# Attention of the first block's layers: V stationary for two heads at once in column halves, outputs turned, probabilities scaled ahead

## The chip, the cores and the metric

The kernel runs on one core of one Trainium2 chip. The metric is the device time of one execution in microseconds; the time given for a kernel is the median of its runs. Of the kernel before there are 3 runs: 1504.77, 1504.91 and 1505.8 us.

## The reference, cut to what matters

Two blocks of two layers each run over 256 rows of 1024 channels, all in float32. The change touches the attention of the first block's two layers (`hybrid_mixer`). There 16 heads of 64 channels stand behind 8 heads that only choose keys: 6 heads of kind A (the best 64 of the keys by those scores), 5 of kind B (a banded mask with a bias), 5 of kind C (a forgetting mask).

```python
def hybrid_mixer(h, cos, sin, w_in, b_in, rel_bias, w_branch, w_out):
    proj = h @ w_in + b_in
    ...
    o_a = dsa_attention(qa, ka, va, qi, ki, wi)
    o_b = chunk_band_attention(qkv_b[:, :, 0], qkv_b[:, :, 1], qkv_b[:, :, 2], rel_bias)
    o_c = forgetting_attention(qkv_c[:, :, 0], qkv_c[:, :, 1], qkv_c[:, :, 2], f_c)
    gates = jax.nn.sigmoid(gate_logits.reshape(B, S, N_BRANCH, D))
    y = (gates[:, :, 0] * (o_a @ w_branch[:WIDTH_A])
         + gates[:, :, 1] * (o_b @ w_branch[WIDTH_A:WIDTH_A + WIDTH_B])
         + gates[:, :, 2] * (o_c @ w_branch[WIDTH_A + WIDTH_B:]))
    return y @ w_out

# each of the three attentions ends so:
    p = jax.nn.softmax(logits, axis=-1).astype(v.dtype)
    out = jnp.einsum('bhqs,bshd->bqhd', p, v)
```

## The kernel before, in words

Rows stand on partitions: 256 rows are two row tiles of 128. Every product with a large weight matrix goes through units. A unit is up to two k-tiles of 128 x 512 weights. SP brings it into a ring of 8 raw buffers, ACT rounds it into a high part (line 1180), POOL subtracts to get the low part (line 674), and PE multiplies three times for each k-tile and row tile: high part of the input by high weights, low by high, high by low (line 716). PE says `unit_used` when it is done, and ACT may run 5 units ahead of PE. SP's order is one list, and PE, ACT, POOL and DVE each run a list of their own with semaphore waits between them.

The attention of a layer is one loop over k (function `attention`, once for each engine), with 24 heads: 8 of kind I, then 5 B, 5 C and 6 A. The dictionary ONE holds its distances: a head h is scored in iteration h+1, its probabilities are turned and weighed with V in iteration h+3. In an iteration PE does, in this order: for even h the score products of two heads (lines 925 and 928, each head on 64 of the 128 array rows); for even k the turning of the queries and keys of the next two heads (line 943); `turn_head` of head k-3, three transposes of its exponentials into a bank (line 904); `weave`, one gate unit of the large products for k up to 23 and branch units for k = 24 to 26; and `weigh_head` of head k-3 (lines 891 to 893). That last one has the turned probabilities as the stationary operand, 128 columns, and 64 columns of V moving, three products for a head, the results in columns 384 to 511 of the same bank.

ACT in an iteration: `prep`, one unit's high part; for (k-6) a multiple of 4 the tanh of a gate chunk; for even k the copy of the turned queries and keys (line 1288); the exponentials of head k-1 in two instructions with their row sums (lines 1300, 1302).

DVE in an iteration: adds mask and scales for head k-1 (lines 1731, 1732), copies the turned probabilities of head k-3 from the bank to SBUF (line 1705); for k a multiple of 4 drains a gate chunk (two adds of 128 x 512); for k = 10 to 17 one round of the choice of the largest 8 (lines 1931 to 1934); and `put_out`: the reciprocal of the row sums (line 1748, for two heads at once) and the product of the head's output with it into `o_rows` (line 1750, 128 x 128). PE's transposes of the following head wait for `head_out`, which this last product gives, since they write the same bank.

The outputs are needed turned, since they are the input of the branch products. `turn_heads` (line 1050) does that with 16 transposes for a layer, in iterations 21, 23, 25, 26 (the dictionary BRANCH_TURNS) and after the loop, each group followed by `heads_hi` on ACT (line 1267) and `heads_lo` on DVE (line 1890), which split it into a high and a low part in `branch_turned` (kinds B and C) or `turned` (kind A).

POOL has, beside the low parts, in layer 0 a modulation sum after every fourth unit (lines 651, 655).

The second block's attention uses the same functions with the dictionaries TWO and other distances.

Of the kernel before, what the change touches and what calls it, by code (L numbers as in the profile page):

```python
# [29 lines left out]
P = 128  # L30
# [69 lines left out]
BRANCH_TURNS = {21: 0, 23: 1, 25: 2, 26: 3}  # L100
# [235 lines left out]
def program(nc, ctx, dram, out, cat, book):  # L336
# [37 lines left out]
    O, _ = place("o_rows", [P, NT, D])  # L374
# [46 lines left out]
    BT, _ = place("branch_turned", [P, 6, 2, S], F32R, at=mb_at)  # L421
    assert mb_at + 6 * 2 * S * 4 <= cm_at + HC * 3 * P * 4
# [39 lines left out]
    ONE = dict(score=1, turn=3, weigh=3, qk=QKT, pt=PT, n_pt=2, n_qk=2, sb=(SB_,), tp=(TP,) * (HI + HB + HC + HA - 2) + SB_, act_copies=False)  # L462
    TWO = [dict(score=3, turn=5, weigh=7, qk=QKT2, pt=PT2, n_pt=3, n_qk=3, sb=(SB_, (0, 2)), tp=tp, act_copies=True)
# [11 lines left out]
    LAST_OF_TURN = (HI + HB + HC - 1,) * 3 + (N_HEADS - 3, N_HEADS - 1)  # L475
# [38 lines left out]
    headed = signal("headed")  # L514
    head_out = signal("head_out")
# [165 lines left out]
    def _(pe):  # L681
# [19 lines left out]
        def unit(c, i, A, tiles=range(NT)):  # L701
# [8 lines left out]
            for m, (a, b) in enumerate(nt):  # L710
                for q, (part, W) in enumerate(((0, HI_), (1, HI_), (0, LO))):
# [3 lines left out]
                    for t in tiles:  # L715
                        ins = pe.matmul(BANK[2 * c["pair"] + t][:, 0:w], A[:, a, part, t * P:(t + 1) * P], W[:, s, b, 0:w],  # L716
                                        start=(i == 0 and m == 0 and q == 0),
                                        stop=(i == len(c["units"]) - 1 and m == len(nt) - 1 and q == 2))
# [160 lines left out]
        def attention(tag, heads, src, weave, pipe):  # L879
# [27 lines left out]
            for k in range(len(heads) + pipe["weigh"]):  # L907
# [22 lines left out]
                if k < len(heads) and k % 2 == 0:  # L930
# [4 lines left out]
                    if one["kind"] == "A" and k - 1 in BRANCH_TURNS:  # L935
                        pe.wait_ge(turned_lo.sem, turned_lo.at((("o", tag), BRANCH_TURNS[k - 1])))
# [8 lines left out]
                if pipe["turn"] == pipe["weigh"]:  # L945
# [54 lines left out]
        for l in range(DEPTH):  # L1000
# [31 lines left out]
            def weave(k, l=l):  # L1032
                if 3 <= k < 3 + HC + 1:
                    forget_products(l, k - 3)
                if k in BRANCH_TURNS:
                    turn_heads(l, BRANCH_TURNS[k])
                if k < 4 * N_GATE:
                    unit(by_key["gate", l, k // 4], k % 4, HT)
# [3 lines left out]

            def turn_heads(l, n):

                pe.wait_ge(head_out.sem, head_out.at((l, LAST_OF_TURN[n])))
                if n:
                    pe.wait_ge(turned_lo.sem, turned_lo.at((("o", l), n - 1)))
                for m, kt in enumerate(((6, 7), (4, 5), (3,), (0, 1), (2,))[n]):
                    for t in range(NT):
                        ins = pe.transpose(BANK[TQ][:, (m * NT + t) * P:(m * NT + t + 1) * P], O[:, t, kt * P:(kt + 1) * P], con("ident"))  # L1050
                ins.then_inc(turned.sem, turned.mark((("o", l), n)))

            def branch_unit(l, cc, b, u):

                pe.wait_ge(turned_lo.sem, turned_lo.at((("o", l), {"C": (1, 0), "B": (2, 1), "A": (3, 4)}[b][u])))
# [23 lines left out]
            turn_heads(l, 4)  # L1079
# [68 lines left out]
    def turned_parts(n):  # L1148

        return ((((BT, 4, 2, 0, P), 0),), (((BT, 1, 1, 0, P), 0), ((BT, 2, 1, 0, DH), 1), ((BT, 3, 1, DH, P), 1)),  # L1150
                (((BT, 0, 1, 0, P), 0),), (((HT, 0, 2, 0, P), 0),), (((HT, 2, 1, 0, P), 0),))[n]
# [15 lines left out]
    def _(act):  # L1167
# [95 lines left out]
        def heads_hi(l, n):  # L1263
# [964 lines left out]
```

## Time and profile before

| | |
|---|---|
| median of 3 runs | 1504.91 us (1504.77 to 1505.8) |
| the profiled execution | 1503.01 us, its span 1501.2 us |
| PE busy | 1464.6 us, 98% |
| DVE, ACT, POOL busy | 771.3, 717.7, 1204.2 us |
| attention loop of layer 0 | about 121 to 235 us in the span |
| attention loop of layer 1 | about 563 to 677 us in the span |
| granted TensorE clock, mean | 0.995 |

The busy share is the time in which an engine has an instruction under way; matmuls are pipelined and their ends are modelled, so a PE that waits a few tenths of a microsecond can still show as busy. Between instructions of the timeline the starts are the safer measure. A float32 matmul of 128 or 256 columns appears as two records, a product of rounded operands or a transpose as one.

### The profile page before, as it was taken

To read this page: it belongs to the slowest core of one execution; us is meant where nothing else is said; L and a number is where in the kernel's file an instruction comes from. 1 tells how busy PE (TensorE), PEld (TensorE's weight loads), DVE (VectorE), ACT (ScalarE), POOL (GpSimd) and SP (SyncE) were. 2 spreads that over 40 slices of the span, in tenths; PEclk is the share of its full clock that TensorE was granted. 3 is DMA by queue.
4 is the path that set the end of the run, shared out by engine and by line. 5 is a ranking of instruction groups with operands and counts; after the bars stand their busy time and mean duration, and the time that the engine had idled before them with its cause. 6 is when DMAs were issued, how large, how long until landed. Compare 5 with 4: busy or idle time off the path is not lost.

```text
span 1501.2 us, 21800 instructions
## 1 busy us (share of the span) xinstructions
PE 1464.6 (98%) x7762; PEld 1237.0 (82%) x7762; DVE 771.3 (51%) x1594; ACT 717.7 (48%) x1154; POOL 1204.2 (80%) x968
## 2 busy tenths in 40 slices
PE   7999999999999999999999999999999999999997
PEld 3898888799978987888788887878888887788886
DVE  7667755666643758655566304264650044555302
ACT  3435554544444444554544444364654345455432
POOL 4799989788878986648898997917999978279994
PEclk9999999999999999999999999999999999999999
DMA  9994546589875995326676565724555657156551
GB/s 354 389 338 169 185 168 215 203 295 330 303 261 169 400 315 168 116 94 203 217 244 204 190 200 165 217 74 137 190 194 196 222 156 225 43 163 202 196 193 60
DMA packets 149685, 313.88 MB, mean 209 GB/s; under 512 B 10933, under 2 KB 31817, under 8 KB 149577
## 3 DMA queue, kind: packets, MB, share of 16 engines
q1 hardware_dynamic: 147824, 311.15, 61.9%
q8 instruction: 62, 1.02, 0.3%
q10 hardware_dynamic: 1754, 1.35, 0.3%
q14 instruction: 45, 0.37, 0.1%
HBM read 311.39 MB, written 1.06 MB: 208 GB/s over the span
## 4 chain that ended last, share of the span: by engine, by line
PE 90%; DVE 5%; ACT 2%; POOL 1%; issue 1%; DMA 0%; SPq 0%; DVEq 0%; ACTq 0%
PE bank L716 56%; PE bank L759 12%; PE bank L760 8%; PE bank L757 5%; PE bank L904 2%; PE bank L925 1%; POOL lo_units L674 1%; PE bank L893 1%; PE bank L892 1%; PE bank L891 1%; PE bank L943 1%; DVE bank L1508 1%; ACT hi_units L1180 1%; PE bank L795 1%; PE bank L847 1%
## 5 line engine op out<-in xcount | busy, mean ns | idle before, releaser
L674 POOL TENSOR_TENSOR lo_units<-raw_units,hi_units 128x512 fp32r<-128x512 f32 (+3 forms) x928 | 1154.0, 1281 | 261.8 <-ACT hi_units L1180 260.5
L1180 ACT ACTIVATE hi_units<-raw_units 128x1024 fp32r<-128x1024 f32 (+1 forms) x470 | 483.2, 1031 | 431.5 <-PE bank L716 274.6
L716 PE MATMUL bank<-hi_units,turned 128*128 128x512 f32 (+3 forms) x1600 | 438.8, 389 | 1.5 <-DVE turned L1556 1.2
L716 PEld LDWEIGHTS bank<-hi_units,turned 128*128 128x128 f32 x1600 | 295.0, 189 | 51.9 <-DVE turned L1556 1.8
L760 PE MATMUL bank<-turned,lo_units 128*128 128x256 f32 x1024 | 288.2, 281 | 0.0
L716 PE MATMUL bank<-hi_units,turned_wide 128*128 128x512 f32 x992 | 274.5, 391 | 0.0
L759 PE MATMUL bank<-turned,hi_units 128*128 128x512 f32 x736 | 260.6, 399 | 0.0
L716 PE MATMUL bank<-lo_units,turned 128*128 128x512 f32 (+3 forms) x800 | 253.3, 384 | 1.5 <-POOL lo_units L674 1.3
L716 PEld LDWEIGHTS bank<-hi_units,turned_wide 128*128 128x128 f32 x992 | 185.3, 188 | 38.5 <-issue 0.5
L760 PEld LDWEIGHTS bank<-turned,lo_units 128*128 128x128 f32 x1024 | 194.2, 190 | 0.2
L716 PEld LDWEIGHTS bank<-lo_units,turned 128*128 128x128 f32 x800 | 150.5, 189 | 31.4 <-POOL lo_units L674 4.8
L759 PEld LDWEIGHTS bank<-turned,hi_units 128*128 128x128 f32 x736 | 138.3, 188 | 34.3
L716 PE MATMUL bank<-lo_units,turned_wide 128*128 128x512 f32 x496 | 160.6, 389 | 0.0
L1508 DVE SCALAR_TENSOR_TENSOR bank<-ada_units,small,bank 128x512 f32<-128x512 f32 x144 | 108.8, 756 | 34.7 <-DMA ada_units<-in_ada_w 30.2
L716 PEld LDWEIGHTS bank<-lo_units,turned_wide 128*128 128x128 f32 x496 | 93.1, 188 | 19.5
L1574 DVE TENSOR_REDUCE bank<-bank 128x256 f32<-128x512 f32 x92 | 64.4, 700 | 86.5 <-PE bank L760 85.6
L757 PE MATMUL bank<-turned,hi_units 128*128 128x256 f32 x576 | 104.0, 283 | 0.0
L757 PEld LDWEIGHTS bank<-turned,hi_units 128*128 128x128 f32 x576 | 90.2, 192 | 0.6
L1300 ACT ACTIVATE scores<-scores,small 128x128 f32<-128x128 f32 x60 | 24.0, 400 | 57.9 <-DVE small L1732 57.3
L2035 DVE SCALAR_TENSOR_TENSOR bank<-x_rows,bank 128x512 f32<-128x512 f32 x8 | 5.2, 693 | 89.7 <-PE bank L716 89.7
L1441 ACT ACTIVATE mlp_relu<-bank 128x256 f32<-128x256 f32 x56 | 21.6, 386 | 60.5 <-DVE bank L1574 59.9
L1570 DVE TENSOR_TENSOR turned_wide<-bank,turned_wide 128x256 fp32r<-128x256 f32 x92 | 39.1, 425 | 15.5 <-ACT turned_wide L1214 12.7
(249 smaller groups left out, 1375.5 us busy)
## 6 DMA issues: line engine op xcount, KB each, us to landing
ada_units<-in_ada_w SPq DMA_DIRECT2D x88, 512.0 KB, 7.4
raw_units<-in_w_ffn_tiles SPq DMA_DIRECT2D x72, 512.0 KB, 5.3
raw_units<-in_mlp_w_out SPq DMA_DIRECT2D x64, 512.0 KB, 3.3
raw_units<-in_mlp_w_tiles SPq DMA_DIRECT2D x56, 512.0 KB, 3.3
raw_units<-in_w_in SPq DMA_DIRECT2D x56, 458.0 KB, 9.7
raw_units<-in_w_in SPq DMA_DIRECT2D x48, 512.0 KB, 6.5
raw_units<-in_w_ffn_out SPq DMA_DIRECT2D x44, 512.0 KB, 3.9
raw_units<-in_moba_w_qkv SPq DMA_DIRECT2D x24, 512.0 KB, 3.7
```

Of the source, the lines that this page charges most:

```text
L674: pool.tensor_tensor(LO[:, s, b, 0:w], RAW[:, u["slot"], b, 0:w], HI_[:, s, b, 0:w].bitcast(F32), ALU.subtract).then_inc(lo_ready.sem, lo_ ...
L716: ins = pe.matmul(BANK[2 * c["pair"] + t][:, 0:w], A[:, a, part, t * P:(t + 1) * P], W[:, s, b, 0:w], start=(i == 0 and m == 0 and q == 0) ...
L757: pe.matmul(bank[:, 0:S], HI_[:, s, b, at:at + P], A[:, kt, part, :], start=kt == 0 and part == 0, stop=False)
L759: pe.matmul(bank[:, :], HI_[:, s, b, at:at + P], A[:, kt, :, :].rearrange("p two s -> p (two s)"), start=kt == 0, stop=False)
L760: ins = pe.matmul(bank[:, 0:S], LO[:, s, b, at:at + P], A[:, kt, 0, :], start=False, stop=kt == KT - 1)
L904: ins = pe.transpose(bank[:, at:at + P], SM[:, h % N_SM, cols], con("ident"))
L1180: act.activation(HI_[:, s, 0:n, 0:w], RAW[:, u["slot"], 0:n, 0:w], ACT.Copy)\
L1300: act.activation(SM[:, h % N_SM, S:S + P], SM[:, h % N_SM, S:S + P], ACT.Exp, bias=NM[:, m:m + 1], scale=-1.0, accum_out=RS[:, m:m + 1])
L1441: act.activation(RTN[:, m % 4, :], BANK[(TQ, TP)[m % 2]][:, 0:S], ACT.Relu).then_inc(act_side.sem, act_side.mark(("relu tile", i, m)))
L1508: ins = v.scalar_tensor_tensor(total, raw[:, k, :], COND[:, kt:kt + 1], partial, ALU.mult, ALU.add)
L1570: tell(v.tensor_tensor(AT[:, n, 1, :], h, AT[:, n, 0, :].bitcast(F32), ALU.subtract), turned_lo, (tag, "tile", n))
L1574: return v.tensor_reduce(to, bank[:, :].rearrange("p (two s) -> p s two", two=2), AX_X, ALU.add)
```

## The change

The products with V swap their operands. V's 64 columns of a head are stationary and the turned probabilities move: for a pair of heads, the first writes partitions 0 to 63 of the bank, the second partitions 64 to 127, 256 columns with the keys of the first tile and 128 columns with those of the second. So the output of a pair comes out turned, and `turn_heads` with its 16 transposes goes. Since rows of queries now lie along the free axis, the division by the row sums can't come behind: DVE takes the reciprocal for each head (in the iteration behind the exponentials), ACT multiplies the exponentials by it in two instructions (`even_probs`), and only then does PE turn them. `pair_hi` and `pair_lo` split a pair's output out of the bank, ACT and DVE, one pair after another in place of the five groups. The product of a pair stands between the two k-tiles of a unit (`amid`), in iterations of even k. The transposes of a pair's second head wait until the copy of the first has left the bank, and those of a pair's first head until `pair_lo` of the pair before. The outputs of kinds B and C move from the place of the masks to that of `o_rows` and the first masks, and the zeroing of two halves moves from k = 19 to k = 14.

```diff
-    ONE = dict(score=1, turn=3, weigh=3, ..., act_copies=False)
+    ONE = dict(score=1, turn=3, weigh=3, ..., act_copies=False, paired=True)
...
+            def weigh_pair(h):
+                if real(h) and h % 2:
+                    bank = BANK[pipe["tp"][h - 1]]
+                    pe.wait_ge(p_turned.sem, p_turned.at((tag, h)))
+                    values = [heads[h - 1 + n]["v"] for n in range(2)]
+                    turned_probs = [pipe["pt"][:, (h - 1 + n) % pipe["n_pt"], :] for n in range(2)]
+                    for n in range(2):
+                        pe.matmul(bank[n * DH:(n + 1) * DH, 0:S], src[:, 0, values[n]:values[n] + DH], turned_probs[n][:, 0:S], start=True, stop=False)
+                    for n in range(2):
+                        ins = pe.matmul(bank[n * DH:(n + 1) * DH, P:S], src[:, 1, values[n]:values[n] + DH], turned_probs[n][:, S:S + P], start=False, stop=True)
+                    ins.then_inc(headed.sem, headed.mark((tag, h)))
             def turn_head(h):
                 if real(h):
-                    pe.wait_ge(exped.sem, exped.at((tag, h)))
-                    if real(tp_user_before(pipe, h)):
+                    if pipe["paired"]:
+                        pe.wait_ge(evened.sem, evened.at((tag, h)))
+                        if h % 2 and pipe["tp"][h - 1] == pipe["tp"][h]:
+                            pe.wait_ge(p_turned.sem, p_turned.at((tag, h - 1)))
+                        elif real(h - 2) and pipe["tp"][h - 2] == pipe["tp"][h]:
+                            pe.wait_ge(turned_lo.sem, turned_lo.at((("o", tag), (h - HI) // 2 - 1)))
...
-                    weave(k)
-                    weigh_head(k - pipe["weigh"])
+                    weave(k, lambda: weigh_pair(k - pipe["weigh"]))
...
-            def turn_heads(l, n):
-                ...
-                for m, kt in enumerate(((6, 7), (4, 5), (3,), (0, 1), (2,))[n]):
-                    for t in range(NT):
-                        ins = pe.transpose(BANK[TQ][:, ...], O[:, t, kt * P:(kt + 1) * P], con("ident"))
...  ACT
+        def pair_hi(l, h):
+            p = (h - HI) // 2
+            act.wait_ge(headed.sem, headed.at((l, h)))
+            for part, lo, hi in pair_parts(p):
+                ins = act.activation(part[lo:hi, 0, :], BANK[ONE["tp"][h - 1]][lo:hi, 0:S], ACT.Copy)
+            ins.then_inc(turned_hi.sem, turned_hi.mark((("o", l), p)))
+        def even_probs(tag, h):
+            act.wait_ge(rows.sem, rows.at(("inverse sums", tag, h)))
+            for m, cols in ((2 * h, slice(S, S + P)), (2 * h + 1, slice(0, S))):
+                ins = act.activation(SM[:, h % N_SM, cols], SM[:, h % N_SM, cols], ACT.Copy, scale=RR[:, m:m + 1])
+            ins.then_inc(evened.sem, evened.mark((tag, h)))
...  (even_probs of head k-2 before the exponentials of head k-1, pair_hi at the end of an even iteration)
...  DVE
+                h = k - pipe["score"] - 1
+                if pipe["paired"] and real(h):
+                    dve.wait_ge(exped.sem, exped.at((tag, h)))
+                    say(v.reciprocal(RR[:, 2 * h:2 * h + 2], RS[:, 2 * h:2 * h + 2]), ("inverse sums", tag, h))
                 weave(k)
...
-                    late(k)
-                    put_out(k - pipe["weigh"])
+                    late(k, outputs)
...  (in late: pair_lo behind the gate drain and ahead of the round of the largest 8)
+            def pair_lo(h, l=l):
+                p = (h - HI) // 2
+                dve.wait_ge(turned_hi.sem, turned_hi.at((("o", l), p)))
+                for part, lo, hi in pair_parts(p):
+                    ins = v.tensor_tensor(part[lo:hi, 1, :], BANK[ONE["tp"][h - 1]][lo:hi, 0:S], part[lo:hi, 0, :].bitcast(F32), ALU.subtract)
+                tell(ins, turned_lo, (("o", l), p))
```

## Rows read from the trace of the kernel before

**Rows 1.** The page: part 1 (busy time by engine) and part 4 (chain of waits).

```profile
PE 1464.6 (98%) x7762; PEld 1237.0 (82%) x7762; DVE 771.3 (51%) x1594; ACT 717.7 (48%) x1154; POOL 1204.2 (80%) x968
...
PE 90%; DVE 5%; ACT 2%; POOL 1%; issue 1%; DMA 0%; SPq 0%; DVEq 0%; ACTq 0%
```

**Rows 2.** Busy time by stretch, layer 0's attention: window, length, PE, PEld, DVE, ACT, POOL.

```profile
150.00:237.00 87.00, 85.85 (x502) 71.88 (x501) 55.88 (x182) 44.06 (x104) 78.43 (x60) 1.00 0.50 167
```

**Rows 3.** Timeline of PE, one pair of iterations in layer 0: start, length, instructions.

```profile
181.87 0.70 PE L925 MATMUL bank<-qk_turned 64*128 64x256 f32 x4
182.41 0.39 PE L928 MATMUL bank<-qk_turned 64*128 64x128 f32 x4
182.72 0.55 PE L904 MATMUL bank<-constants,scores 128*128 128x128 f32 x3
183.03 1.17 PE L716 MATMUL bank<-hi_units,turned 128*128 128x512 f32 x4
...
185.86 0.33 PE L891 MATMUL bank<-proj_rows,probs_turned 128*128 128x64 f32 x2
...
186.48 0.61 PE L943 MATMUL bank<-constants,proj_rows 128*128 128x128 f32 x4
187.18 0.52 PE L904 MATMUL bank<-constants,scores 128*128 128x128 f32 x3
187.46 1.17 PE L716 MATMUL bank<-hi_units,turned 128*128 128x512 f32 x4
...
190.29 0.33 PE L891 MATMUL bank<-proj_rows,probs_turned 128*128 128x64 f32 x2
...
191.00 0.70 PE L925 MATMUL bank<-qk_turned 64*128 64x256 f32 x4
```

**Rows 4.** Timeline of DVE in the same stretch.

```profile
182.92 0.29 DVE L1731 CUSTOM_DVE_ANT_0 scores<-bank,forget_masks 128x128 f32<-128x128 f32 x1 [0.58 <-PE bank L928]
...
183.60 0.56 DVE L1705 COPY probs_turned<-bank 128x384 f32<-128x384 f32 x1
184.19 0.62 DVE L1931 MAX8 small<-idx_scores 128x8 f32<-128x256 f32 x2
...
185.63 0.18 DVE L1748 RECIPROCAL small<-small 128x4 f32<-128x4 f32 x1
186.75 0.29 DVE L1750 TENSOR_TENSOR o_rows<-bank,small 128x128 f32<-128x128 f32 x1 [0.94 <-PE bank L893]
```

**Rows 5.** Timeline of PE: transposes of the outputs, and the loop's last iterations.

```profile
210.51 0.60 PE L1050 MATMUL bank<-constants,o_rows 128*128 128x128 f32 x4
210.87 1.16 PE L716 MATMUL bank<-hi_units,turned 128*128 128x512 f32 x4
...
224.58 0.52 PE L904 MATMUL bank<-constants,scores 128*128 128x128 f32 x3 [0.54 <-DVE o_rows L1750]
...
236.67 1.18 PE L716 MATMUL bank<-hi_units,branch_turned 128*128 128x512 f32 x4
```

**Rows 6.** Timeline of PE: two float32 products of 256 columns on the whole array.

```profile
152.83 0.60 PE L1070 MATMUL bank<-constants,small 128*128 128x256 f32 x2
153.26 0.59 PE L1071 MATMUL bank<-constants,small 128*128 128x256 f32 x2
```

**Rows 7.** Timeline of ACT: exponentials, a high part, the split of an output.

```profile
183.60 0.40 ACT L1300 ACTIVATE scores<-scores,small 128x128 f32<-128x128 f32 x1 [3.04 <-DVE small L1732]
...
184.49 1.04 ACT L1180 ACTIVATE hi_units<-raw_units 128x1024 fp32r<-128x1024 f32 x1
...
229.09 0.39 ACT L1267 ACTIVATE branch_turned<-bank 128x256 fp32r<-128x256 f32 x1 [2.00 <-PE bank L1050]
```

**Rows 8.** Timeline of DVE: the split of the same output.

```profile
229.58 0.42 DVE L1890 TENSOR_TENSOR branch_turned<-bank,branch_turned 128x256 fp32r<-128x256 f32 x1
```

**Rows 9.** Timeline of POOL around the end of layer 0's loop.

```profile
227.17 2.51 POOL L674 TENSOR_TENSOR lo_units<-raw_units,hi_units 128x512 fp32r<-128x512 f32 x2 [2.67 <-ACT hi_units L1180]
...
235.70 1.29 POOL L674 TENSOR_TENSOR lo_units<-raw_units,hi_units 128x512 fp32r<-128x512 f32 x1
```

More of the change, by code:

```diff
@@ L373, in program @@
     X, _ = place("x_rows", [P, NT, D])
-    O, _ = place("o_rows", [P, NT, D])
+    O, o_at = place("o_rows", [P, NT, D])
     HT, turned_at = place("turned", [P, KT, 2, S], F32R)
@@ L420, in program @@
     CM, cm_at = place("forget_masks", [P, HC, 3 * P])
[L421 to L422 removed]
+    WHOLE, _ = place("branch_turned", [P, 4, 2, S], F32R, at=o_at)
+    MIXED, _ = place("mixed_turned", [P, 2, 2, S], F32R, at=mb_at)
+    assert 4 * 2 * S * 4 <= NT * D * 4 and mb_at + 2 * 2 * S * 4 <= cm_at
+    BT = [WHOLE[:, 0], WHOLE[:, 1], MIXED[:, 0], MIXED[:, 1], WHOLE[:, 2], WHOLE[:, 3]]
     ADA_M, _ = place("ada_units_2", [P, NC, UNIT_K, CW], at=pt_at)
@@ L699, in pair_free, with unit @@
                 pe.wait_ge(drained.sem, drained.at(c["before"]))
-        def unit(c, i, A, tiles=range(NT)):
+        def unit(c, i, A, tiles=range(NT), amid=None):
             u = c["units"][i]
@@ L710, in unit @@
             for m, (a, b) in enumerate(nt):
+                if amid and m == len(nt) - 1:
+                    amid()
                 for q, (part, W) in enumerate(((0, HI_), (1, HI_), (0, LO))):
@@ L715, in unit @@
                     for t in tiles:
-                        ins = pe.matmul(BANK[2 * c["pair"] + t][:, 0:w], A[:, a, part, t * P:(t + 1) * P], W[:, s, b, 0:w],
+                        ins = pe.matmul(BANK[2 * c["pair"] + t][:, 0:w], (A[a] if A is BT else A[:, a])[:, part, t * P:(t + 1) * P], W[:, s, b, 0:w],
                                         start=(i == 0 and m == 0 and q == 0),
@@ L1289, in attention @@
                             .then_inc(qk_turned.sem, qk_turned.mark((tag, p)))
+                if pipe["paired"] and HI <= k - pipe["score"] - 1 < len(heads):
+                    even_probs(tag, k - pipe["score"] - 1)
                 h = k - pipe["score"]
@@ L1310, in attention @@
                         .then_inc(p_turned_act.sem, p_turned_act.mark((tag, h)))
-                if heads[0]["kind"] == "I" and k in BRANCH_TURNS:
-                    heads_hi(tag, BRANCH_TURNS[k])
+                if pipe["paired"] and h >= HI and h % 2:
+                    pair_hi(tag, h)
         def bias_rows(l):
@@ L1926, in late @@
                     tell(v.tensor_tensor(GATES[:, 1, j * CW:(j + 1) * CW], banks[1][:, :], b, ALU.add), drained, key)
+                h = k - ONE["weigh"]
+                if h >= HI and h % 2:
+                    pair_out(h)
                 r = k - (HI + 2)
@@ L1958, in branch_out @@
                 tell(ins, drained, key)
-            attention(l, heads_one(), mask_of, weave, ONE, scaled_output(l), late)
-            heads_lo(4)
+            attention(l, heads_one(), mask_of, weave, ONE, pair_lo, late)
             branch_out(1, "C")
```

63 lines of the change are left out of this document (22 added, 41 removed).

## The prediction, written before the changed kernel was seen

> **What bounds the kernel now.** Read the page's busy times first, then the chain of waits: PE is busy 98% of the span and makes 90% of the chain, and no other engine has more than 5% of that [rows 1]. So what counts is PE's own stream of instructions, and for everything else only whether it makes PE wait. The table of stretches says the same of the place that is changed: in 150 to 237 us PE is busy 85.9 of 87 us at full granted clock, and DVE and ACT 64% and 51%; POOL has 78.4 of 87 and must be watched [rows 2]. Then read the timeline of PE start to start, since modelled ends hide short waits. The reader is to see there that a pair of iterations takes 9.13 us (181.87 to 191.00), as scores 0.85, turning of probabilities 0.31, unit 2.83, weighing 0.62, turning of queries and keys with a wait 0.70, probabilities 0.28, unit 2.83, weighing with what follows 0.71 [rows 3].
>
> **The change part by part.** The sum is made for one layer; both layers issue the same instructions, so it counts twice.
>
> Removed, weighing. A head's three products take 0.62 us (185.86 to 186.48); 190.29 to 191.00 is 0.09 longer, which I put down to the change to half-height tiles, and which stays [rows 3]. 16 heads: 9.9 us. These products are bound by their loads: a 256-column record costs 0.215 us [rows 6], so six of 64 columns would stream in 0.32 us, but take 0.62, about 0.10 a record for 128 stationary columns.
>
> Removed, a wait. In even iterations four transposes of queries and keys come before `turn_head`. Four such transposes take 0.36 us (210.51 to 210.87) [rows 5], but here 0.70 pass (186.48 to 187.18), because DVE's `put_out` of the head before ends at 187.04 [rows 3, 4]. That is 0.34 us in six iterations (k = 12 to 22) and 0.54 us at k = 24, which the page shows as idle [rows 5]: 2.6 us. What is late next there is the copy of the turned probabilities (before a second head) or `pair_lo` (before a first one); both are timed below.
>
> Removed, `turn_heads`: 16 transposes at 0.36 us for four [rows 5], 1.4 us. In all 13.9 us go from PE.
>
> Added on PE, eight products of pairs. One has four records of 256 columns and four of 128, in two column halves. One after another they stream in 4 x 0.215 + 4 x 0.107 = 1.29 us [rows 6]; with perfect overlap in 0.64. No row shows column halves. The nearest is the score block, with the same eight records in row halves: 0.85 us from its first start to that of the transposes [rows 3], so overlap works there with 0.2 us of loads and switching on top; its entry cost 0.09. For column halves I take 0.9 us: 0.85 + 0.09, less a little since a load has 64 columns rather than 128. Ends: 0.7 (overlap and hardly a switch) and 1.5 (1.29 + 0.2 for two switches). 8 x 0.9 = 7.2 us. Net 6.7 us a layer.
>
> The same eight-record block speaks for overlap in the terms of the Trainium skill. Its page TensorEngine Tiling (Array Packing), section Tiling Modes, lets tiles load and multiply in parallel and says that a change of mode drains the array; this block in the trace agrees in row halves. Against the change stands the page TensorE: Matmul & The Clock Gate, Part 3: a weight load overlaps matmuls under way only when the row group differs, and column halves share all rows. By that rule the loads would stand bare; it is a rival below.
>
> Added waits, steady state. Let an even iteration start at 0. The new pair of iterations is 9.13 - 0.62 - 0.62 - 0.34 + 0.9 = 8.45 us. PE: queries and keys to 0.36, second head's transposes to 0.66, half a unit, the pair's product at 2.1 to 3.0, half a unit to 4.45, scores to 5.3, first head's transposes of the next pair at 5.3. ACT's `pair_hi`, 0.39 us [rows 7], can start about 3.2; DVE's `pair_lo`, 0.42 us [rows 8], ends about 4.2. PE needs it at 5.3: 1.1 us to spare. On DVE behind it stand the choice of the largest 8 (184.19 to 185.63, 1.44 us), the reciprocal 0.2, mask 0.68, copy 0.59, another 1.44 + 0.2 + 0.68 + 0.59 [rows 4]: the copy of the second head ends at 4.2 + 5.8 = 10.0, and the product wants it at 8.45 + 2.1 = 10.55. 0.5 to spare, and only while the choices run; afterwards 3. DVE loses 16 `put_out` of 0.29 and gets eight more reciprocals, and the splits are the same data, so it has no more work than before.
>
> ACT gets two scaled copies a head. No row has them; the exponentials of the same tiles, with their reads of the sums, take 0.89 us (183.60 to 184.49) [rows 7], and without the reads 0.7. Ends 0.6 and 0.9; I take 0.7. Per pair of iterations ACT then has high parts 2 x 1.0, exponentials 2 x 0.89, copies of queries and keys 0.6, scaling 2 x 0.7, `pair_hi` 0.4, and every other time a tanh of the size of a high part, 1.0: 6.2 or 7.2 of 8.45 us. The scaled head is ready about 2 us before PE turns it. So in the loop I price this at 0. At the end it has a price: ACT is held by `pair_hi` of the pair at k = 24, whose product comes after the whole unit (at 3.2 to 4.1 after the iteration's start), until 4.6, then makes a high part to 5.6 and scales the last head to 6.3; PE wants to turn it at 5.85. Wait 0.5 us a layer.
>
> POOL, layer 0. ACT's delay at k = 24 puts the high part for the unit that POOL starts at 227.17 to 5.6 us after the start of iteration 24; before it was 3.1 (the iteration starts at 224.58 - 0.54) [rows 5, 9]. Behind that unit stand a modulation sum (to 235.70, 6.0 us) and a single low part: 14.2 and 15.5 after the start. PE wants that one at 15.6 and the next, ready at 16.7, at 17.0. No wait by a few tenths; I allow 0.2. Layer 1 has no such sums. The memory's new places and the earlier zeroing (in k = 14, where DVE would otherwise wait for `pair_hi`) cost nothing: if that cover fails, 1 us once a layer. SP's list is the same; what it waits for comes with PE.
>
> Sum: 2 x (13.9 - 7.2 - 0.5) = 12.4, less 0.2 for POOL and 0.2 for small waits: 12.0 us. The profiled execution took 1503.0 us (span 1501.2), so 1491.0; the median of the runs is 1.9 us above it, hence 1504.9 - 12.0 = 1492.9 us.
>
> **Rivals.**
> - B, no overlap in column halves: 1.5 us in place of 0.9, 16 times 0.6 = 9.6 us lost, 1502.5 us. For it: no row shows this mode. Against: the row halves overlap.
> - C, part of the overlap: eight loads of 64 columns stand bare, at half of 0.10 us each 0.4 us a pair, 6.4 us in all: 1499.3 us. Against it: loads hide behind matmuls in all of PE's units now. The rule of the Trainium skill (TensorE: Matmul & The Clock Gate, Part 3) would give this case. The same time comes out if DVE's 0.5 us of room is gone and the pairs stall by some 0.4 us.
> - D, slower: ACT and DVE close a ring. `pair_hi`, `pair_lo`, choice of the largest 8, reciprocal, scaling, exponentials, high part, tanh, copy of queries and keys, scaling, exponentials, `pair_hi`: 0.5 + 1.44 + 0.2 + 0.8 + 0.9 + 1.0 + 1.0 + 0.6 + 0.7 + 0.9 + 0.4 = 8.4 us with a tanh, 7.4 without, on average 7.9 against PE's 8.45. It decides above 8.45; the gain is gone at about 9.6 (9.13, with the 0.15 us of `turn_heads` that each pair saves, and what the loop's two ends save). At 10.0 the six pairs lose 0.7 us each and the ends give back 1.3: 3 us a layer, 1511 us. For it: five handovers a round. Against: the waits that stand before these steps now are of 3 us [rows 7].
>
> **How the numbers follow.** Forecast 60%, C 17%, B 15%, D 8%. The likeliest gives 1493 us. Low end: 0.75 for the pair's product and no waits, 1489.5. High end 1502.0, which takes in C and a part of B; left out are most of B and D. About 0.2% (3 us) is what a measurement of this kernel can tell from no change; that is 1501.9 and below for faster. Forecast, C and a little of B: 80% faster; most of B: 12% same; D: 8% slower.
>
> **What would show it.** In PE's timeline: the pair's eight records take about 0.9 us from first start to the unit's next product (1.3: C; 1.5: B); 0.36 us between the turning of queries and keys and `turn_head`; pairs of iterations 8.45 us apart; some 0.5 us of idle time before the transposes of k = 26, on ACT; no `turn_heads` line. On ACT: scaled copies of 0.3 and 0.4 us. Outside the two loops stretches of the same length. I am wrong if PE's idle time before line 904 in the new numbering exceeds 3 us in a layer, if the product of a pair is over 1.2 us, or if POOL's low parts hold PE by more than 1 us behind layer 0's loop.

## The result, and the profile after

The changed kernel takes 1495.47 us (median of 6 runs, 1495.1 to 1497.33) beside 1505.02 us (6 runs, 1504.72 to 1506.75) of the kernel before on the same chip: 0.9944 of it, 95% interval 0.9934 to 0.9955. The forecast was 12.0 us less; it came to 9.5 us less, inside the range. The profiled execution took 1497.33 us, its span 1495.5, which is 5.7 us below the span of before. It is the slowest of the six runs, so its losses are at the upper end of what they show.

One correction to the text ahead of the prediction: the zeroing moves to the iteration `HI + HB + score + 1` = 15, not 14. It matters below.

The page of the changed kernel, busy time by engine (share, instructions) and the chain of waits by engine, answers to [rows 1]:

```profile
PE 1457.5 (97%) x7666; PEld 1218.3 (81%) x7666; DVE 785.5 (53%) x1582; ACT 739.3 (49%) x1222; POOL 1203.5 (80%) x968
...
PE 86%; DVE 9%; ACT 2%; issue 1%; POOL 1%; DMA 0%; SPq 0%; DVEq 0%; ACTq 0%
```

PE has 7.1 us less to do, ACT 21.6 more, and DVE's share of the chain has gone from 5 to 9%: something holds PE on DVE's side. The same stretch as [rows 2], changed kernel (window, length, PE, PEld, DVE, ACT, POOL, granted clock, DMA share, GB/s):

```profile
150.00:237.00 87.00, 86.10 (x474) 65.55 (x473) 55.31 (x180) 58.79 (x143) 79.90 (x62) 1.00 0.49 167
```

In the attention loop PE stays busy, ACT goes from 44 to 59 us and is still not the bound. Now PE's timeline of the changed kernel, one pair of iterations without a wait (start, length, instructions), against [rows 3]:

```profile
172.32 0.70 PE L949 MATMUL bank<-qk_turned 64*128 64x256 f32 x4
...
176.32 0.60 PE L965 MATMUL bank<-constants,proj_rows 128*128 128x128 f32 x4
176.75 0.49 PE L928 MATMUL bank<-constants,scores 128*128 128x128 f32 x3
177.00 1.17 PE L720 MATMUL bank<-hi_units,turned 128*128 128x512 f32 x4
178.00 0.61 PE L720 MATMUL bank<-lo_units,turned 128*128 128x512 f32 x2
178.55 0.65 PE L908 MATMUL bank<-probs_turned,proj_rows 128*64 128x256 f32 x4
179.03 0.39 PE L910 MATMUL bank<-probs_turned,proj_rows 128*64 128x128 f32 x4
179.35 1.21 PE L720 MATMUL bank<-hi_units,turned 128*128 128x512 f32 x4
180.40 0.62 PE L720 MATMUL bank<-lo_units,turned 128*128 128x512 f32 x2
180.95 0.70 PE L949 MATMUL bank<-qk_turned 64*128 64x256 f32 x4
```

A pair takes 172.32 to 180.95 = 8.63 us; 8.45 was forecast and 9.13 is before. The pair's product passes in 0.80 us (178.55 to 179.35). Two other differences belong to it: the two low products ahead of it take 0.55 us to its start where a pair of them takes 0.46 elsewhere (entry, 0.09), and the four high products behind it take 1.05 us where they take 0.91 elsewhere (their first load starts only with them, 0.14). So it costs 1.02 us in all, not 0.9: this unit takes 3.95 us (177.00 to 180.95), a unit without the block 2.84, and 0.09 of the difference is the entry of the scores, which was there before. Queries and keys pass in 0.43 us (176.32 to 176.75), not 0.36.

From the first score in iteration 11 to the last branch product, layer 0's loop went from 85.45 to 80.56 us and layer 1's from 86.08 to 80.28: 10.7 us together. The span fell by only 5.7. So 5.0 us were lost where nothing was edited, and the largest piece is in one row. DVE's timeline of the changed kernel (start, length of the group):

```profile
441.89 1.42 DVE L1548 TENSOR_TENSOR mod_rows<-bank,row_vectors 128x512 f32<-128x512 f32 x2
443.34 23.95 DVE L1606 TENSOR_TENSOR bank<-x_rows,mod_rows 128x512 f32<-128x512 f32 x2
467.32 0.70 DVE L1670 SCALAR_TENSOR_TENSOR bank<-bank,mod_rows 128x512 f32<-128x512 f32 x1
```

The same two products in the kernel before:

```profile
446.90 2.77 DVE L1587 TENSOR_TENSOR bank<-x_rows,mod_rows 128x512 f32<-128x512 f32 x2
```

POOL in the changed kernel meanwhile:

```profile
426.33 39.80 POOL L676 TENSOR_TENSOR lo_units<-raw_units,hi_units 128x512 fp32r<-128x512 f32 x32 [2.63 <-ACT hi_units L1190]
```

and in the kernel before:

```profile
428.63 40.70 POOL L674 TENSOR_TENSOR lo_units<-raw_units,hi_units 128x512 fp32r<-128x512 f32 x32 [3.07 <-ACT hi_units L1180]
```

And what follows on PE, with the table of stretches around it (changed kernel, columns as in [rows 2]):

```profile
471.23 1.11 PE L799 MATMUL bank<-constants,o_rows 128*128 128x128 f32 x4 [2.57 <-DVE o_rows L1696]
```

```profile
468.00:472.00 4.00, 1.43 (x8) 0.97 (x7) 3.23 (x7) 1.88 (x4) 0.94 (x1) 0.90 0.00 0
472.00:476.00 4.00, 4.00 (x17) 3.25 (x16) 1.71 (x3) 2.06 (x3) 3.42 (x4) 0.67 0.00 0
```

The reader is to see a DVE instruction with two inputs in SBUF (`x_rows`, `mod_rows`), 0.7 us long when POOL rests, that lasts 23.3 us (with its twin 23.95). It ends 0.6 us after POOL's unbroken row of 32 low parts, which ends at 466.13. The row alone does not explain it: in the kernel before, the same two products start 18 us into an equally unbroken row of 32 low parts and take 1.07 and 1.78 us. PE then waits 2.57 us, is busy 1.43 of 4 us, and runs at its lower level, 1.2 GHz, for a part of the next 4 us (granted clock 0.67 in the mean). The lead over the kernel before goes from 3.6 us at 438 to 0.6 us behind it at 474.

### The profile page after: what moved, and what is told of

The parts are those of the page before. It is cut to its first block, busy times and chain, and to the rows that moved or that the text cites. A ratio compares the mean times of both kernels' runs of the same rounds, so it can differ in the third digit from the quotient of the medians.

```text
span 1495.5 us, 21644 instructions
## 1 busy us (share of the span) xinstructions
PE 1457.5 (97%) x7666; PEld 1218.3 (81%) x7666; DVE 785.5 (53%) x1582; ACT 739.3 (49%) x1222; POOL 1203.5 (80%) x968
## 4 chain that ended last, share of the span: by engine, by line
PE 86%; DVE 9%; ACT 2%; issue 1%; POOL 1%; DMA 0%; SPq 0%; DVEq 0%; ACTq 0%
PE bank L720 53%; PE bank L763 12%; PE bank L764 8%; PE bank L761 5%; DVE bank L1606 2%; PE bank L949 1%; PE bank L928 1%; POOL lo_units L676 1%; PE bank L965 1%; ACT hi_units L1190 1%; PE bank L908 1%; PE bank L799 1%; DVE bank L1527 1%; PE bank L851 1%; PE bank L1000 0%
## 5 line engine op out<-in xcount | busy, mean ns | idle before, releaser
L2058 DVE SCALAR_TENSOR_TENSOR bank<-x_rows,bank 128x512 f32<-128x512 f32 x8 | 5.2, 692 | 89.7 <-PE bank L720 89.7
L1460 ACT ACTIVATE mlp_relu<-bank 128x256 f32<-128x256 f32 x56 | 21.6, 386 | 60.4 <-DVE bank L1593 59.8
L2071 DVE SCALAR_TENSOR_TENSOR bank<-x_rows,bank 128x512 f32<-128x512 f32 x8 | 5.6, 696 | 75.8 <-PE bank L720 75.6
```

Source lines behind the costliest of these rows:

```text
L1460: act.activation(RTN[:, m % 4, :], BANK[(TQ, TP)[m % 2]][:, 0:S], ACT.Relu).then_inc(act_side.sem, act_side.mark(("relu tile", i, m)))
```

## The experiments

All were run beside the kernel before, whose medians were 1503.57 us in the first session (after_port, before_port, serial, moved), 1503.85 in the second (twice, unscaled, before_amid, beside) and 1503.66 in the third (zero_only, moved_all, beside_all). `after_port` is the changed kernel with one edit elsewhere. All others contain that edit too: those made from the changed kernel are read against `after_port`, `before_amid` against `before_port`. Across sessions only the ratios are compared. "Loops" is the time of both layers' loops in the trace, each from the first score in iteration 11 to the first transposes behind the branch products.

| kernel | median us (runs) | of before, 95% interval | span us | loops us |
|---|---|---|---|---|
| kernel before | 1505.02 (6) | | 1501.2 | 172.0 |
| changed kernel | 1495.47 (6) | 0.9944 (0.9934 to 0.9955) | 1495.5 | 161.3 |
| after_port | 1492.74 (5) | 0.9928 (0.9915 to 0.9942) | 1491.4 | 161.2 |
| before_port | 1502.15 (12) | 0.9989 (0.9980 to 0.9997) | 1501.7 | 171.9 |
| serial | 1503.63 (10) | 1.0000 (0.9988 to 1.0011) | 1501.7 | 172.2 |
| twice | 1503.98 (10) | 0.9998 (0.9989 to 1.0007) | 1504.4 | 173.6 |
| unscaled | 1492.93 (4) | 0.9928 (0.9915 to 0.9942) | 1493.9 | 162.0 |
| before_amid | 1500.77 (8) | 0.9977 (0.9967 to 0.9987) | 1498.2 | 170.1 |
| zero_only | 1492.64 (5) | 0.9932 (0.9919 to 0.9944) | 1492.9 | 160.9 |
| moved | 1490.12 (4) | 0.9915 (0.9902 to 0.9928) | 1487.8 | 159.9 |
| beside | 1492.62 (5) | 0.9921 (0.9907 to 0.9934) | 1489.7 | 159.3 |
| moved_all | 1491.29 (5) | 0.9919 (0.9905 to 0.9933) | 1488.5 | 159.9 |
| beside_all | 1488.09 (4) | 0.9900 (0.9887 to 0.9914) | 1488.5 | 159.3 |

### Was it the port? after_port, before_port

"Port" stands for the theory that a DVE instruction with two inputs in SBUF can't run while POOL works on SBUF. The edit takes one of the two inputs out of SBUF.

```diff
-  x = x + bank                    # both row tiles; then bank = x * mod, two inputs in SBUF
+  bank = x + bank; x = bank       # only in the FFN's output product, chunk 0 of layer 0
+  bank = bank * mod               # one input in SBUF
```

> The changed kernel, with one step of VectorE rewritten at the end of layer 0's feed-forward (the first output half): the row sum is made in the bank, copied to x_rows, and the scaling reads the bank, so that no instruction there reads two operands from SBUF while GpSimd runs. Same result. Theory (port): in the changed kernel's trace the product of x_rows and mod_rows took 23.3 us there (0.7 us when undisturbed), while GpSimd ran without a gap, and PE then waited 2.6 us and ran one stretch at half clock; with the edit that product takes 0.7 us, PE does not wait at about 470 us, the lead over the kernel before that stood at 3.6 us at 433 us of the span is kept, and the trace ends 4 us earlier than the changed kernel's own trace (about 1491.5 us of span). The median falls by as much as the stall is in the timed runs, 0 to 4 us: 1491.5 to 1495.5. Rival (artefact): the long record is only a late end and PE waited for its own product; then the wait of 2.6 us stays and the span is 1495.

> The kernel before with the same rewritten step. Theory (port): there the two products took 2.8 us in the one trace and PE did not wait, since VectorE had 18.6 us to spare; if the long block is a matter of luck in each run, the median falls by up to 2 us from 1505.0 (to 1503.0, the time of its profiled run, in which the block was short) and the runs lie closer together. Rival: the kernel before never has the block, and the median stays within 0.5 us of 1505.0. In both cases after_port against before_port gives the change without this luck: by the two traces' loops alone 4.8 + 5.4 = 10.2 us.

DVE's timeline of after_port at the place:

```profile
441.51 1.29 DVE L2008 COPY x_rows<-bank 128x512 f32<-128x512 f32 x2
442.83 1.42 DVE L1548 TENSOR_TENSOR mod_rows<-bank,row_vectors 128x512 f32<-128x512 f32 x2
444.28 1.30 DVE L2013 TENSOR_TENSOR bank<-bank,mod_rows 128x512 f32<-128x512 f32 x2
```

The same arithmetic with one input in SBUF takes 1.30 us for both, PE no longer waits at 468, and the span is 4.1 us shorter. Before_port's span moved by 0.5 us the other way. So the block and the clock behind it are shown for the traced execution. What a median run pays is not: the intervals of changed kernel and after_port overlap (1.6 thousandths apart, 2.4 us), and before_port's median too is below that of before, by 1.4 us, as the expectation had it for a block that comes and goes. With the same edit on both sides the change is worth 10.3 us in the traces and 9.4 in the medians, and without it on either side 5.7 in the traces and 9.5 in the medians.

### Do the column halves overlap? serial, twice

```diff
 serial: both heads of a pair in column half 0, one head after the other (the outputs are overwritten)
-  pe.matmul(bank[n * DH:(n + 1) * DH, 0:S], ...)
+  pe.matmul(bank[0:DH, 0:S], ...)
 twice: the eight products issued twice
+  for _ in range(2):
```

> after_port with both heads of a pair written to column half 0 of the array (partitions 0 to 63), one head behind the other, so that nothing can overlap; the output of the odd heads is overwritten and the result is not the reference's. Theory (column halves overlap): the eight records now take 0.80 us from first start to the next unit's start; without overlap 1.29 us of streaming plus the same overhead of 0.16, 1.45 us, 0.65 us more for each of 16 pairs: 10 us slower than after_port, so at the time of the kernel before. Rival (the halves don't overlap, and the 0.80 us is a modelled or shorter stream): the block and the time stay as they are.

> after_port with each pair's eight records issued twice in a row (same result, since the second pass starts the sums anew). It prices the bare stream of a pair's product, without a change of tile mode. Theory (overlap, and the mode changes cost the rest): a pass in the middle adds 0.65 to 0.75 us for each of 16 pairs, 10.4 to 12 us in all, so of the 1.03 us that a pair's product costs in the changed kernel about 0.33 are entry, exit and the following unit's first loads. Rival (loads stand bare, the Trainium skill's page TensorE: Matmul & The Clock Gate, Part 3: a load overlaps only under another row group): a pass has 0.64 us of stream and eight loads of 64 columns at 0.05 us, 1.04 us, 16.6 us in all.

PE's timeline of serial, and of twice:

```profile
178.93 0.65 PE L908 MATMUL bank<-probs_turned,proj_rows 128*64 128x256 f32 x2
179.41 0.38 PE L909 MATMUL bank<-probs_turned,proj_rows 128*64 128x128 f32 x2
179.63 0.59 PE L908 MATMUL bank<-probs_turned,proj_rows 128*64 128x256 f32 x2
180.06 0.38 PE L909 MATMUL bank<-probs_turned,proj_rows 128*64 128x128 f32 x2
180.38 1.20 PE L720 MATMUL bank<-hi_units,turned 128*128 128x512 f32 x4
```

```profile
188.64 0.65 PE L909 MATMUL bank<-probs_turned,proj_rows 128*64 128x256 f32 x4 [0.28 <-DVE probs_turned L1725]
189.12 0.39 PE L911 MATMUL bank<-probs_turned,proj_rows 128*64 128x128 f32 x4
189.34 0.60 PE L909 MATMUL bank<-probs_turned,proj_rows 128*64 128x256 f32 x4
189.77 0.39 PE L911 MATMUL bank<-probs_turned,proj_rows 128*64 128x128 f32 x4
190.09 1.19 PE L720 MATMUL bank<-hi_units,turned 128*128 128x512 f32 x4
```

In one half the block takes 1.45 us (178.93 to 180.38) where two halves take 0.80, and a pair of iterations 9.27 where it was 8.63: +0.64, sixteen times 10.2 us. The loops are 11.0 us longer and the span 10.3; about 1.0 us of that is a longer wait in k = 18 of layer 0 (period 10.67), which has another cause (below). The overlap is shown to be complete, for the second pass in twice costs 0.65 us a pair (period 9.28), and eight records one after another would be 1.29 by [rows 6]. Rival B is out, and so is C in its first form: with bare loads a pass would cost 1.04. (Twice's time also holds a wait of 1.4 us in k = 18 in both layers, so only its period of 9.28 is read.) Of the 1.02 us of a pair's product, 0.65 is the stream and 0.37 goes to entry, exit and the loads behind.

### Does the scaling cost anything? unscaled

```diff
 (the probabilities stay undivided; ACT's two scaled copies a head and their wait are left out)
-  pe.wait_ge(evened.sem, evened.at((tag, h)))
+  pe.wait_ge(exped.sem, exped.at((tag, h)))
```

> after_port without the scaling ahead: no reciprocals on VectorE, no scaled copies on ScalarE, PE turns the bare exponentials as soon as they are there. The outputs aren't divided by the row sums, and the result is not the reference's. Theory (the scaling is hidden but for the loop's end): PE's wait of 0.27 us at k = 26 goes, VectorE has 0.4 us more room in a pair of iterations so that its waits in 16 and 18 go too; 0.5 to 2.5 us in all below after_port. Rival D (ScalarE and VectorE close a ring around the scaling): the waits before the transposes go and 5 us or more come back.

1492.93 us against 1492.74: nothing to gain. The waits in k = 16 and 18 are there as before in layer 0 (periods 8.97 and 9.12); the one at k = 26 is gone, and PE waits 0.33 us for a low part of POOL's at 235.57 instead. So 21 us of additional work on ACT are hidden, and rival D (a ring over ACT) is out. The 0.5 to 2.5 us expected here were not seen: its span is 2.5 us longer than after_port's, 1.1 us of it one pair of layer 1 at 10.06 us where after_port has 8.91 (explained below).

### What makes the two waits? moved, zero_only

The changed kernel's periods in layer 0 are 8.66, 8.63, 8.97, 9.07, 8.63, 8.63 us. The two long ones have a wait each, which PE's timeline of the changed kernel shows:

```profile
187.53 0.65 PE L908 MATMUL bank<-probs_turned,proj_rows 128*64 128x256 f32 x4 [0.27 <-DVE probs_turned L1724]
...
196.60 0.65 PE L908 MATMUL bank<-probs_turned,proj_rows 128*64 128x256 f32 x4 [0.36 <-DVE probs_turned L1724]
```

and DVE's timeline what stands ahead of that copy:

```profile
183.45 0.48 DVE L1940 MEMSET mixed_turned<- 64x512 f32 x1 [0.17 <-DVE probs_turned L1724]
184.08 0.48 DVE L1941 MEMSET mixed_turned<- 64x512 f32 x1
...
186.92 0.56 DVE L1724 COPY probs_turned<-bank 128x384 f32<-128x384 f32 x1
...
189.32 0.86 DVE L1914 TENSOR_TENSOR mixed_turned<-bank,mixed_turned 64x256 fp32r<-64x256 f32 x2 [0.53 <-ACT mixed_turned L1278]
...
194.56 0.51 DVE L1963 TENSOR_SCALAR idx_scores<-idx_scores 128x384 f32<-128x384 f32 x1
...
195.98 0.56 DVE L1724 COPY probs_turned<-bank 128x384 f32<-128x384 f32 x1
```

```diff
 zero_only and moved: the zeroing in k = 20 (15 in the changed kernel, 19 in the kernel before)
-  if k == HI + HB + ONE["score"] + 1:
+  if k == HI + HB + HC + ONE["score"] + 1:
 moved alone: the last comparison of the choice one iteration later
-  if r == TOPK // 8 - 1:
+  if r == TOPK // 8:
     link(v.tensor_scalar(IDX[:, :], IDX[:, :], PICKED, NEG, ALU.not_equal, ALU.mult))
```

> after_port with two VectorE steps moved out of the stretch in which it is full: the zeroing of the two halves from iteration 15 back to 19, and the last step of the choice of the 64 keys (a comparison over 128 x 384, 0.51 us) from iteration 17 to 18. Same result. Theory (full VectorE): the waits of PE before the pairs' products in iterations 16 and 18 (0.34 and 0.44 us in layer 0) come from the zeroing (1.3 us) and from the comparison with the two-part split of the third pair; both go, 0.8 us a layer, 1.6 us in all against after_port. Rival: PE waits there for ScalarE's scaled probabilities, and nothing changes.

> after_port with the zeroing alone back in k = 19, the last comparison left in k = 17. Theory: the two waits of the pair products on the copy of turned probabilities (0.27 us in k = 16 and 0.36 us in k = 18, periods 8.97 and 9.07) come from 1.3 us of zeroing in k = 15 for the first and partly for the second: then both shrink, the first period is 8.63 and the second 8.63 to 8.8; the time lies 0.8 to 1.4 us below after_port. Rival: the two-part split of the third pair and the comparison make them, and they stay: no change against after_port.

Zero_only: k = 16 runs without a wait (8.63), but k = 18 then waits 0.67 us:

```profile
196.46 0.65 PE L908 MATMUL bank<-probs_turned,proj_rows 128*64 128x256 f32 x4 [0.67 <-DVE probs_turned L1724]
```

In layer 0 its six periods sum to 52.55 us, after_port's to 52.56. Measured from the start of the pair of k = 15 and 16, the product of k = 16 and the third pair's split both come 0.3 us earlier than in after_port, so the theory on the first wait held. What took the gain back is the comparison: it lasts 0.81 us here and 0.49 in after_port. In layer 1 it lasts 0.36 us in both; there the wait of k = 16 is gone and nothing comes in its place (8.63 for 8.97, and 8.91 in k = 18 as in after_port), and the loop is 0.34 us shorter. The 0.8 to 1.4 us expected did not come, and the two medians are the same.

The comparison has one input in SBUF and writes SBUF, and its length sets the period of k = 18 across all traces that have it in k = 17 and a pair's product of 0.8 us: 0.36 us goes with periods of 8.91 to 8.93, 0.49 to 0.51 with 9.05 to 9.07, 0.57 with 9.12, 0.81 with 9.37 and 1.49 with 10.06. The timelines of DVE and POOL show what makes it long, first in unscaled, then in the changed kernel, both in layer 1:

```profile
634.08 1.49 DVE L1960 TENSOR_SCALAR idx_scores<-idx_scores 128x384 f32<-128x384 f32 x1
634.06 2.64 POOL L676 TENSOR_TENSOR lo_units<-raw_units,hi_units 128x512 fp32r<-128x512 f32 x2 [1.64 <-ACT hi_units L1190]
```

```profile
635.95 0.36 DVE L1963 TENSOR_SCALAR idx_scores<-idx_scores 128x384 f32<-128x384 f32 x1
635.96 1.51 POOL L676 TENSOR_TENSOR lo_units<-raw_units,hi_units 128x512 fp32r<-128x512 f32 x1 [1.66 <-ACT hi_units L1190]
```

Where POOL starts 0.02 us ahead, the comparison takes 1.49 us; where DVE is 0.01 us ahead, it takes 0.36 and POOL's low part 1.51 in place of 1.24. Twice (1.49 and 1.51 us) and serial (1.48 in layer 0) have their long pairs of 10.7 us from the same. So the changed kernel's 0.30 us in k = 18 of layer 1 is partly luck: by unscaled it could have been 1.4. That POOL is the cause is read from these starts; no run moves POOL.

Moved has all periods at 8.62 to 8.66, 0.7 us a layer less than after_port, 1490.12 us: taking the comparison out of k = 17 is what frees k = 18, and in k = 18 it takes 1.37 us in layer 0 without making PE wait. Moved's interval lies below the changed kernel's; it overlaps that of after_port, so of the 2.6 us between these two medians the traces' loops show 1.4.

### How much had been reachable with less? before_amid

```diff
 (the kernel before, its six products of a head between the unit's two k-tiles, not behind them)
-  weave(k)
-  weigh_head(k - pipe["weigh"])
+  weave(k, lambda: weigh_head(k - pipe["weigh"]))
```

> The kernel before with one thing moved: the two products of a head's weighing, operands as before, stand between the two k-tiles of the unit rather than behind it (iterations up to 23). Everything else, turn_heads and put_out too, is as before. Theory: the waits of PE for head_out (0.34 us in six even iterations and 0.54 us at k = 24 of each layer, 2.6 us a layer) go, since VectorE has the second half of the unit for put_out: 4 to 5.2 us faster than before, which is the part of the change's gain that the place alone gives. Rival: VectorE's round of the choice of the largest 8 stands ahead of put_out, so the waits stay in iterations 12 to 16, and only 2 us are gained.

PE's timeline of before_amid, to be read beside 186.48 and 187.18 of [rows 3]:

```profile
186.04 0.60 PE L945 MATMUL bank<-constants,proj_rows 128*128 128x128 f32 x4
186.47 0.49 PE L906 MATMUL bank<-constants,scores 128*128 128x128 f32 x3
```

The wait on the head's output is gone in this pair (0.43 instead of 0.70 us; 0.3 us of such waits are left in layer 0, 1.0 in layer 1), which also shows that 0.43 is what four such transposes cost in this place. The pair fell by 0.16 us only, to 8.97: the four high products behind the inserted ones take 1.01 us (184.56 to 185.57) where they took 0.91, in both units, and the unit's last low products take 0.54 to the scores where they took 0.46 to the products. Expected were 4 to 5.2 us. Against before_port, which has the same edit elsewhere, the ratios differ by 1.2 thousandths, 1.8 us, with intervals that overlap; the loops are 1.8 us shorter and the span 3.5. So about a sixth of the 10.7 us that the whole change gives in the loops comes from the place of the products alone.

### Is there more? beside, moved_all, beside_all

Beside puts the pair's product right ahead of the scores, both in half-array modes, so that the array goes back to whole tiles once. Moved_all and beside_all also have the one-input form in the attention's output product of both layers.

```diff
 beside
-  turn_head(...); weave(k, lambda: weigh_pair(k - pipe["weigh"]))
+  # odd k: turn_head between the unit's k-tiles; even k: ahead of the unit
+  weave(k, ...); weigh_pair(k - pipe["weigh"])
 moved_all, beside_all
-  one_input = key == ("ffo", 0, 0)
+  one_input = coef is not None
```

> moved with another order on PE: the pair's product stands at the end of the even iteration's unit, right before the score block, so that PE goes from column halves to row halves without a full-array unit between; and the transposes of the next pair's first head stand between the two k-tiles of the odd iteration's unit, which gives pair_hi and pair_lo the time that this takes away. Same result. Theory (each change of tile mode costs): one of three changes a pair goes, 0.1 to 0.25 us for 14 pairs, 1.5 to 3.5 us below moved. Rival 1 (the price is the drain, whichever modes meet): no difference. Rival 2: VectorE, whose copy of the first head now comes 1.5 us later in each odd iteration, becomes late in iterations 12 to 18 and PE waits; 1 to 4 us above moved.

> The kernel 'moved' with the one-SBUF-input form also in the first half of the attention's output product (wout, chunk 0) of both layers: there too DVE multiplies into the bank, adds X in the bank, copies to X, and multiplies the bank, so no DVE instruction of that step has two SBUF inputs. The theory that the shared port holds DVE there: the products of 2.4 us at 267 and 2.7 us at 701 in after_port fall to 0.7 us for two, two copies of 0.6 us each come ahead, so each step gets 0.5 to 1.3 us shorter, and PE's wait behind the output product (1.34 us at 278 in the changed kernel) falls to about 0.3. Time: 1 to 2 us below moved, 1488 to 1489. Rival: the long products there are the price of the data's way and not of the port: they stay, the copies come on top, and the time is 1 us above moved.

> The kernel 'beside' (pair product right ahead of the scores) with the same one-SBUF-input form in wout's first half. If beside's -0.4 us a layer in the loops is real and only what lies outside took it back by the alignment of DVE with POOL, this one is 0.5 to 1 us below moved_all, near 1488. Rival: the earlier product brings nothing in sum, the two are the same within 0.5 us.

DVE's timeline of moved, then of moved_all:

```profile
262.14 1.28 DVE L2004 TENSOR_TENSOR x_rows<-x_rows,bank 128x512 f32<-128x512 f32 x2
...
266.38 3.02 DVE L1606 TENSOR_TENSOR bank<-x_rows,mod_rows 128x512 f32<-128x512 f32 x2
```

```profile
263.43 1.29 DVE L2008 COPY x_rows<-bank 128x512 f32<-128x512 f32 x2
...
267.67 1.30 DVE L2013 TENSOR_TENSOR bank<-bank,mod_rows 128x512 f32<-128x512 f32 x2
```

The blocked products fall from 3.02 to 1.30 us for two, so the port holds them here too, but two copies of 1.29 come ahead and PE's wait behind falls from 1.34 to 0.96, not to 0.3. The 0.4 us are gone again at 427, where PE's loads wait 0.6 us for POOL, and the span is 0.7 longer; moved_all is no faster than moved. The mechanism held and the time expected from it did not come: 1.7 us saved for 1.3 us spent is no gain.

Beside has pairs of 8.51 us, 0.12 less, with one at 8.90; its loops are 0.3 us a layer shorter than moved's. The 1.5 to 3.5 us expected did not come: its span is 1.9 us longer than moved's, and the ratios (0.9921 and 0.9915) tell no difference. Beside_all has the lowest median of the study, 1488.09, but its span equals moved_all's and its interval overlaps those of moved and moved_all. That it beats the kernel before and the changed kernel is shown, that it beats moved is not.

## Why the prediction was right, and where it was off

The mechanism was right: the weighing, its waits and `turn_heads` go from PE (13.9 us a layer by the sum, 0.4 too much since the waits were 0.27 us and not 0.34), the eight paired products come, and the scaling hides. Of 12.0 us forecast, the loops gave 10.7 in the traces. By its own steps:

- **The pair's product, 0.9 us.** It is 1.02 with its two edges. The step took the score block's 0.85 us plus the entry, and gave a bit back for the narrower loads; the 0.14 us by which the four high products behind it are longer was left out. 16 times 0.12 us: 1.9 us too little.
- **Queries and keys, 0.36 us.** The [rows 5] transposes of the outputs were taken for the price of those of queries and keys, which take 0.43 where nothing waits. With the product it explains the pair: 8.45 + 0.12 + 0.07 = 8.64, measured 8.63. Six or seven times a layer, 0.9 us in both.
- **"0.5 us to spare" on DVE for the second head's copy, and the zeroing at nothing.** This is the step whose reasoning failed. The zeroing was thought to stand where DVE would wait for `pair_hi`; it stands one iteration later, and 1.3 us pass from the end of the copy ahead of it to the next choice. The third pair's split in two parts was not costed at all ([rows 8] has one part of 0.42 us; two take 0.86, and ACT's before them 0.77), nor was the comparison, 0.51 us here and up to 1.5 when POOL is ahead of it. PE pays 0.34 and 0.44 us in layer 0, 0.34 and 0.30 in layer 1: 1.4 us in all, and `moved` gets them back.
- **k = 26, 0.5 us.** 0.27 us, on ACT's scaled copy, as said. POOL's price of 0.2 us was not there: the table of waits from 224 to 262 us names no wait of PE on POOL. In layer 0 the stretch behind the last score gained 2.2 us where these steps gave 1.6.
- **What the sum did not know.** In the kernel before, layer 1 had a second wait on a head's output, which the six rows of layer 0 did not show:

```profile
637.70 0.52 PE L904 MATMUL bank<-constants,scores 128*128 128x128 f32 x3 [0.71 <-DVE o_rows L1750]
```

  It makes that pair 9.74 us long where the others take 9.13. Ahead of it the comparison takes 1.48 us (from 635.54, POOL's low part from 635.52), in layer 0 0.36. So 0.6 us of the gain in layer 1 is a comparison that POOL held in one trace and not in the other: luck, and not the change.
- **"Outside the two loops stretches of the same length."** Wrong, by 5.0 us in the traces, 4.1 of them the one held DVE product. The change shifts POOL's and DVE's later work against each other; which shift makes the hold is open, since the row of 32 low parts was there before too. In the medians the forecast is 2.5 us off: the loops explain 1.3 of that. For the rest the port is not shown, since with the same edit on both sides the medians still differ by 9.4 us only.

Rival C's second form (DVE's room gone, the pairs stall by 0.4 us) came true for two pairs of six. The three bounds beyond which I would have been wrong were not reached: PE's waits before the transposes (0.27 us a layer), the product's 1.2 us, POOL's 1 us.

The Trainium skill's page TensorE: Matmul & The Clock Gate, Part 3, has the sentence that a weight load overlaps matmuls under way only when the row group differs. The runs contradict it for column halves: 0.65 us a pass, where 0.64 is perfect overlap.

## What to carry to other kernels

When two narrow outputs can share the array in column halves, count the longer half's stream and some 0.4 us for each block's edges. Two blocks of half tiles side by side gave 0.12 us a pair in the traces and nothing that the medians show. When a step is moved into a busy iteration, redo the budget of the engine for that very iteration, with every one-time step in it; the average pair has room that one pair has not. And look, at the place of the edit and outside it, for DVE instructions that read and write SBUF beside GpSimd work, those with two SBUF inputs above all: hundredths of a microsecond in the starts can decide whether one takes 0.4 or 1.5 us.

## What the runs showed of the hardware

- **A DVE product can be held for 23.3 us.** The Trainium skill's page SBUF — State Buffer, section SBUF: two separate sides, has a DVE instruction with two SBUF inputs contend with a GpSimd instruction that reads SBUF; whichever starts first holds the shared ports for its whole instruction. The traces agree on which instructions: products from SBUF and SBUF take 1.07 to 3.4 us beside POOL and 0.7 alone, those from the bank 0.65 to 0.7. But here the hold did not last one instruction of POOL, 1.24 us (39.80 / 32), but until the row of them ended, some 18 of them. In before, beside an equal row, the same two products took 1.07 and 1.78 us. Which meeting of starts decides that, no run tells.
- **A DVE comparison with one SBUF input meets POOL too.** The same instruction over 128x384 takes 0.36 us when it starts ahead of POOL's and up to 1.5 us when it starts 0.02 us behind; the hold then ends with the one instruction of POOL.
- **A wait of 2.57 us has a price behind it.** With PE busy 1.43 of 4 us, the granted clock of the next 4 us was 0.67; four transposes took 1.11 us there and 0.66 us at the same step elsewhere.
- **Column halves cost nothing in overlap and 0.37 us in edges** a block: 0.09 at the entry, 0.14 in the loads behind, the rest at the exit. Not all of it belongs to the half tiles: in before_amid, whose inserted products use the whole array, the four high products behind take 1.01 us in place of 0.91.
